# A gated convolution layer: how the inverse root mean squares of the first 512 positions are spread over the partitions

## The reference

```python
def conv_mixer(h, w_in, conv_w, conv_b, ln_g, ln_b, w_out):
    a, b, gate = jnp.split(h @ w_in, 3, axis=-1)
    u = a * jax.nn.sigmoid(b)
    u = causal_depthwise_conv(u, conv_w) + conv_b      # 31 taps
    u = layer_norm(u) * ln_g + ln_b
    return (jax.nn.silu(u) * jax.nn.silu(gate)) @ w_out
out = x + conv_mixer(rms_norm(x, norm_g), ...)
```

## Time and profile before

| | us |
|---|---|
| median of 3 executions | 356.94 |
| lowest and highest | 356.31, 358.1 |
| the profiled execution, its own time | 358.03 |
| its span, first to last instruction | 356.2 |

### The profile page before, as it was taken

How to read it: one execution, slowest core, us unless ns; L and a number is a source line. 1 busy time by engine, 2 the same in 40 slices (tenths; PEclk the granted TensorE clock), 3 DMA queues, 4 the chain that set the end, 5 groups by cost and what they waited for, 6 DMA issues and landing times.

```text
span 356.2 us, 4758 instructions
## 1 busy us (share of the span) xinstructions
PE 349.8 (98%) x1564; PEld 290.3 (81%) x1564; DVE 320.8 (90%) x514; ACT 232.1 (65%) x334; POOL 269.1 (76%) x194
## 2 busy tenths in 40 slices
PE   8999999999999999999999999999799999999996
PEld 7878888888888888888888888888688888888886
DVE  4779799999999999989999998995799989998962
ACT  6989685668847871998658876966664962442400
POOL 0129999999999998889999999884887541359140
PEclk9999999999999999999999999999899999999999
DMA  7995011202411321404121213223723595056052
GB/s 245 411 413 220 36 59 59 95 26 68 108 61 30 89 61 59 118 2 118 59 63 35 82 59 67 101 70 90 251 74 121 197 418 210 1 162 224 29 204 91
DMA packets 30521, 43.51 MB, mean 122 GB/s; under 512 B 18337, under 2 KB 18849, under 8 KB 30497
## 3 DMA queue, kind: packets, MB, share of 16 engines
q1 hardware_dynamic: 30352, 43.21, 36.1%
q10 hardware_dynamic: 144, 0.00, 0.0%
HBM read 34.82 MB, written 4.19 MB: 110 GB/s over the span
## 4 chain that ended last, share of the span: by engine, by line
PE 36%; DVE 26%; issue 16%; POOL 13%; ACT 7%; DMA 1%; SPq 0%; ACTq 0%; DVEq 0%; POOLq 0%
DVE acc L1187 20%; PE acc L713 12%; PE mm L713 9%; PE mm L634 7%; PE mm L651 6%; POOL pconv L1496 4%; POOL w_lo L1440 3%; POOL x_lo L1429 3%; ACT prod L870 2%; DVE stats L1195 2%; DMA raw<-w_in 1%; POOL pool_before L1496 1%; POOL u L1474 1%; ACT acc L852 1%; DVE u L1154 1%
## 5 line engine op out<-in xcount | busy, mean ns | idle before, releaser
L634 PE MATMUL mm<-x_hi,w_hi 128*128 128x512 f32 x352 | 137.8, 392 | 0.0
L634 PE MATMUL mm<-x_hi,w_lo 128*128 128x512 f32 x352 | 137.5, 390 | 0.0
L634 PE MATMUL mm<-x_lo,w_hi 128*128 128x512 f32 x352 | 137.4, 390 | 0.0
L1187 DVE SCALAR_TENSOR_TENSOR acc<-u,chan,acc 128x512 f32<-128x512 f32 x157 | 110.8, 751 | 0.1
L634 PEld LDWEIGHTS mm<-x_hi,w_lo 128*128 128x128 f32 x352 | 66.4, 188 | 13.9
L634 PEld LDWEIGHTS mm<-x_hi,w_hi 128*128 128x128 f32 x352 | 66.4, 189 | 13.7
L1496 POOL TENSOR_TENSOR pconv<-pconv,prod 128x512 f32<-128x512 f32 x60 | 76.6, 1295 | 1.3 <-ACT prod L870 1.3
L634 PEld LDWEIGHTS mm<-x_lo,w_hi 128*128 128x128 f32 x352 | 66.4, 189 | 13.5
L1187 DVE SCALAR_TENSOR_TENSOR acc<-u,w_sum,acc 128x512 f32<-128x512 f32 x90 | 67.7, 752 | 2.4 <-ACT acc L852 2.2
L870 ACT ACTIVATE prod<-u,chan 128x512 f32<-128x512 f32 x69 | 47.9, 715 | 19.9 <-POOL pconv L1496 18.4
L1440 POOL TENSOR_TENSOR w_lo<-raw,w_hi 128x1024 fp32r<-128x1024 f32 (+1 forms) x21 | 49.4, 2354 | 8.8 <-ACT w_hi L819 8.7
(11 more groups left out here) (109 smaller groups left out, 536.1 us busy)
## 6 DMA issues: line engine op xcount, KB each, us to landing
raw<-w_in SPq DMA_DIRECT2D x22, 512.0 KB, 3.3
nat<-x_t SPq DMA_DIRECT2D x16, 256.0 KB, 6.1
sgate<-x SPq DMA_DIRECT2D x8, 512.0 KB, 10.5
raw<-w_out SPq DMA_DIRECT2D x8, 512.0 KB, 3.3
nat<-x SPq DMA_DIRECT2D x8, 512.0 KB, 7.4
y<-nat SPq DMA_DIRECT2D x15, 256.0 KB, 2.2
raw_late<-w_out SPq DMA_DIRECT2D x4, 512.0 KB, 4.0
sig<-w_out SPq DMA_DIRECT2D x4, 512.0 KB, 4.0
```

Source lines behind the costliest of these rows:

```text
L634: ins = nc.tensor.matmul(bank(("unit", m, h)), w[:, m % 3, k, :], xx[:, k, half(h)], start=(k == 0 and i == 0), stop=(k == KC - 1 and i == 2))
L1187: ins = nc.vector.scalar_tensor_tensor(dst, chain_in(j, chain, k), tap(j, chain, k), chain_bank(j, chain), ALU.mult, ALU.add)
```

## The change

The spread of half 0 is done as that of half 1: two products of 512 columns from rounded diagonals. ScalarE still makes the four diagonals of half 0, now rounded to fp32r and into `diags[:, 0]`; since half 1's product reads the same tile, ScalarE first waits for that product (`rms_all_ready`). VectorE makes the four low parts: three between `make_hn(1, 6)` and `make_hn(1, 7)`, the fourth after `make_hn(1, 7)`. The place of the spread in TensorE's list stays the same.

```diff
             def spread_rms(h):
 
+                spread = rms_spread(h).rearrange("p (t q) -> p t q", t=TPH)
                 if h == 1:
-                    spread = rms_spread(1).rearrange("p (t q) -> p t q", t=TPH)
                     pe.wait_ge(ones_r_ready, 1)
-                    pe.wait_ge(diag_hi_ready, TPH)
-                    nc.tensor.matmul(spread, ones_r[:], diags[:, 0, :, :], start=True, stop=False)
-                    pe.wait_ge(diag_lo_ready, TPH)
-                    ins = nc.tensor.matmul(spread, ones_r[:], diags[:, 1, :, :], start=False, stop=True)
-                else:
-                    for i in range(TPH):
-                        pe.wait_ge(diag_ready, i + 1)
-                        ins = nc.tensor.matmul(rms_spread(0)[:, i * P:(i + 1) * P], ones[:], diag(i), start=True, stop=True)
-                ins.then_inc(rms_all_ready, 1)
+                pe.wait_ge(diag_hi_ready, TPH * (NH - h))
+                nc.tensor.matmul(spread, ones_r[:], diags[:, 0, :, :], start=True, stop=False)
+                pe.wait_ge(diag_lo_ready, TPH * (NH - h))
+                nc.tensor.matmul(spread, ones_r[:], diags[:, 1, :, :], start=False, stop=True).then_inc(rms_all_ready, 1)
...
             def rms_diagonal(t):
 
                 act.wait_ge(ident_in, 16)
+                act.wait_ge(rms_all_ready, 1)
                 act.wait_ge(rms_ready, rms_count(t))
-                nc.scalar.activation(diag(t), ident[:], ACT.Copy, scale=rms[:, t:t + 1]).then_inc(diag_ready, 1)
+                nc.scalar.activation(diags[:, 0, t, :], ident[:], ACT.Copy, scale=rms[:, t:t + 1]).then_inc(diag_hi_ready, 1)
...
                 dve.wait_ge(rms_ready, rms_count(t))
-                i = t - TPH
-                nc.vector.tensor_scalar(diags[:, 0, i, :], ident[:], rms[:, t:t + 1], None,
-                                        ALU.mult).then_inc(diag_hi_ready, 1)
-                dve.wait_ge(diag_hi_ready, i + 1)
+                i = t % TPH
+                if t >= TPH:
+                    nc.vector.tensor_scalar(diags[:, 0, i, :], ident[:], rms[:, t:t + 1], None,
+                                            ALU.mult).then_inc(diag_hi_ready, 1)
+                dve.wait_ge(diag_hi_ready, (i if t >= TPH else t + TPH) + 1)
                 nc.vector.scalar_tensor_tensor(diags[:, 1, i, :], ident[:], rms[:, t:t + 1],
                                                diags[:, 0, i, :].bitcast(F32), ALU.mult,
                                                ALU.subtract).then_inc(diag_lo_ready, 1)
...
             finish_w_lo()
-            for k in range(6, KC):
-                make_hn(1, k)
+            make_hn(1, 6)
+            for t in range(TPH - 1):
+                rms_diagonal(t)
+            make_hn(1, 7)
+            rms_diagonal(TPH - 1)
             scale_gate(0, 0)
```

More of the change, by code:

```diff
@@ L201, in gated_conv_layer @@
         ones_r_ready = sem("ones_r_ready")
-        diag_ready = sem("diag_ready")
         diag_hi_ready = sem("diag_hi_ready")
@@ L460, in half @@
             return slice(h * HALF, (h + 1) * HALF)
-        def diag(i):
-            return sgate[:, i, 0:P]
         def words(columns):
```

## The result

| | before | after |
|---|---|---|
| median, us | 356.94 (7 executions, 356.23 to 358.17) | 359.41 (7 executions, 358.68 to 360.42) |
| profiled execution, its own time | 358.03 | 358.68 |
| its span | 356.2 | 356.8 |
| span less the start of the means' spread (line 694, now 684) | 356.2 - 253.94 = 102.3 | 356.8 - 256.20 = 100.6 |

The changed kernel takes 1.0058 times the time of before, 95% interval 1.0034 to 1.0082: about 2.1 us more. (This is not the quotient of the two medians, which lie 2.47 us apart.) The last line of the table has to be read first. The two profiled spans differ by only 0.6 us because TensorE's clock fell behind the wait for the means in the one execution and not in the other. Up to the means the changed kernel is 2.26 us later. Its profile is also the fastest of its seven executions, while that of before is among the slower ones.

What follows compares the result with a forecast made beforehand. Bound by a chain through GpSimd that starts when half 0's spread ends, not by TensorE (98% busy). Spread 2.7 us late, clock taken as no net change: median 356.94 to 359.6 us, profiled 358.03 to 360.7; range 356.9 to 361.4.

Steps and rivals of the forecast that it cites:

- What sets the end: Half 0's spread: when it ends counts, not its TensorE time; GpSimd has 0.1 us reserve before its start at 43.52.
- TensorE: At the spread: eight narrow passes cost 0.90 us, two wide products 0.45, so 0.45 us less if operands are there.
- ScalarE: Four rounded diagonals of half 0: still 1.31 us; the added wait for half 1's product costs nothing.
- VectorE and GpSimd: Low parts beside finish_x_lo alternate with GpSimd; the fourth ends at 39.02, the spread at 39.57, 2.7 us later.
- What is late next: After the spread: copy_rms(0) near 39.6, unit 4's weights on GpSimd 46.2 for 43.52; the shift goes to the end.
- The clock: TensorE's clock likely falls near 39 us, losing 1.6 us, 0.5 left at the end; net shift 3.2, 1.6 or 2.7.
- GpSimd did not get in first: Rival at 34.53 against 34.59: GpSimd issues first, three low parts each wait; +3.5 us, 360.4; chance 0.20.
- Little blocking: Rival at the low parts: only the fourth waits for one GpSimd instruction; spread end 37.3, +0.4, 357.3; chance 0.11.
- no blocking: Rival at the low parts: 0.35 us each beside GpSimd, spread ends 36.90, time 356.9, not slower; chance 0.14.
- The arrival of TensorE's saving: Rival: low parts early and TensorE setting the end all along; -0.45 us, 356.5; chance 0.03.

Runs made afterwards that it cites:

- Experiment 2: Kernel before, only the eight narrow passes of half 0's spread moved twelve matmuls later in TensorE's list (k = 6 for k = 2); ratio to before 1.0126.
- experiment 3: Changed kernel, its two wide products nine matmuls later in TensorE's list (k = 5), so TensorE works while VectorE is blocked; ratio to before 1.0112.
- Experiment 8: Kernel before plus VectorE's four low parts at their places in the changed kernel, read by nothing, narrow passes kept; ratio to before 1.0043.
- 4: Changed kernel, GpSimd made to wait for the four low parts before its x_lo of half 1, k = 2; ratio to before 1.0089.
- 10: Kernel before with nine filling matmuls in TensorE's wait for the means and its narrow passes one channel block earlier (k = 1); ratio to before 0.9976.
- experiment 6: Changed kernel with nine filling matmuls, results overwritten, on TensorE ahead of the means' spread; ratio to before 1.0076.
- experiment 1: Changed kernel, half 0's four low parts reading the identity from a copy in PSUM, so each has one SBUF input; ratio to before 1.0012.
- experiment 9: Changed kernel with its wide products nine matmuls later (k = 5) and eighteen filling matmuls ahead of the means; ratio to before 1.0052, median 359.26 us.

## Why the prediction was right

**What sets the end.** Right: the end of the spread, not the time that it takes on TensorE. Experiment 2 moved the one without the other and got 2.69 us for 2.7; experiment 3 gave TensorE 2.1 us back and gained nothing. Experiment 8 adds that the blocked low parts by themselves, with the spread on time, make VectorE and the end 1.1 us late. The condition that goes with it, no reserve on GpSimd, was shown from both sides (4: late costs 1.80; 10: early gains nothing).

**TensorE.** Right: one pitch of 0.23 for the high product (35.83 to 36.06), and the next matmul 0.34 behind a late one (38.61 to 38.95). The saving of 0.45 us did not come about in the changed kernel, since the low product came late; that time gained on TensorE ahead of the means ends in a longer wait for them is shown by experiment 3.

**ScalarE.** Right: the four rounded diagonals took 1.33 us for 1.31, and the added wait doesn't show.

**VectorE and GpSimd.** Right in mechanism, order and place: the first low part ahead by 0.06 us, then turns, each blocked low part ending 0.15 behind a GpSimd instruction, until k = 5 was missing. The size was off a little. From one GpSimd end to the next I had 1.38 us (0.22 and 1.16), taken from blocks of 512 columns; it was 1.28 and 1.27, and the fourth low part ended 0.16 behind GpSimd for 0.22. So the fourth low part ended at 38.56 and not 39.02: 0.18 of that is the earlier start of the stretch, 0.28 these terms. The spread was 2.25 late, or 2.4 from VectorE's start, for 2.7.

**What is late next.** Right: `copy_rms(0)` 39.14 for 39.6, unit 4's weights 45.76 for 46.2, and the shift of 2.25 kept to the means. That all engines shift together was so in this profile; VectorE's waits stayed at 1.1 and TensorE's at 2.17.

**The clock.** Half right. I had a fall at 39 us as likely; in the profile of the change there is none (clock 1.0, behind a standstill of 2.3 us, 36.29 to 38.61, for 3.0 forecast; the profile, which counts from the end of a matmul, has 2.16), while it is there in experiment 6, and there its sizes came out. From `make_hn(1, 6)` to the last matmul ahead of the means it was 221.46 us for 219.95 in the changed kernel, 1.5 lost for the 1.6 forecast; 0.4 of it was left at the means for 0.5; and TensorE's wait for them would have been 1.1 without the filling, for 1.05. I had not seen that the fall at the means, which the profile of before has, is missing in more than half of the executions of the same kernel. The table shows what that does to a single pair of profiles: 2.26 us at the means became 0.6 us of span. The forecast for the changed kernel's profiled execution, 360.7 us, came out at 358.68 mostly for that reason. The one for the median, 359.6, came out at 359.41, a rise of 2.47 us for 2.7, and that this is so near is in part luck: it adds 2.7 us to a median of three executions, and five of the seven executions of the changed kernel had a mean clock of 0.995, while by their times three of the seven of the kernel before are in the slower group. The forecast knew nothing of these odds.

**The rivals.** GpSimd did not get in first. Little blocking and no blocking are out by 1.39 and 1.36 us beside an `x_lo`, and by experiments 1 and 8. The arrival of TensorE's saving is out because its low parts were not early, and experiment 3 shows that time gained there does not arrive. What no blocking would have given is seen in experiment 1, where the ratio's interval holds 1.

**Open.** Of the changed kernel's own seven executions five had a mean clock of 0.995 (359.04, 359.15 and three from 360.16 to 360.42), and it isn't told which of the two waits the clock fell behind in each. By how much the clock's odds widen or narrow 1.0058 is therefore not settled. They don't make the cost: experiments 9 and 10, of which neither has a fall, lie 2.85 us or 0.8% apart. Why that is 0.3 us more than the 2.59 at the means isn't settled either; both are read from single profiles on the one side and medians on the other, and the executions of experiment 9 alone lie up to 1 us apart.

## What to carry to other kernels

Before an instruction is put on VectorE, count its inputs in SBUF and look what GpSimd does at that moment: beside a run of long GpSimd instructions, a two-input instruction of 0.35 us can wait for most of a GpSimd instruction (1.39 and 1.36 us here), and reading a constant from a copy in PSUM takes that away. A saving on the engine that is 98% busy is worth nothing where that engine waits later; what counts is the time at which its result is there. And where TensorE has a wait of some 2 us, compare profiles ahead of it, because a single execution on either side may hold a fall of the clock as large as the change.

## What I had not expected of the hardware

The same wait of 2.15 to 2.17 us ahead of the means left TensorE at 2.4 GHz in one execution and put it at 1.2 GHz for a while in another; over 29 executions of the kernel before, 17 and 12 had the one and the other. This makes two groups of times, 1.4 to 1.9 us apart by their medians on the three chips, and nine matmuls whose result is thrown away merge them into the faster one. They are not free everywhere: in experiment 6, where TensorE came late, they cost 0.8 us. Behind waits of 4.3 to 4.5 us the part from the means to the end took 102.8 and 103.1 us, for 102.2 or 102.3 where the clock fell behind waits of 2.2 to 3.9, and 100.6 or 100.7 where it did not.
